# Sparse scores over stacked two-part operands, MLP up products grouped by part, tables in shared buffers, and a few unread products

## The chip, the cores and the metric

The kernel runs on one core of a Trainium2 chip. The metric is the device time of one execution in microseconds; the time of a kernel is the median of its runs.

## The reference, cut to what matters

The program computes, for one sequence of 256 positions and a width of 1024, three blocks one after another, each with a mixer and an MLP: a first block (softmax attention with a forget gate beside retention, with an adaptive norm from a condition vector), a block with sparse attention beside a pooling mixer, and a block with gated linear attention. All inputs are float32. The MLPs, and the sparse attention that the change rewrites, are:

```python
def sqrelu_mlp(x, w1, w2):                      # w1 1024x4096, w2 4096x1024
    return jnp.square(jax.nn.relu(x @ w1)) @ w2
...
q = h[..., :o1]...                              # 8 heads of 64, in 2 groups
k_cmp, v_cmp, k_slc, v_slc, k_win, v_win = ...  # of each group
kc = compress_blocks(k_cmp, ...)                # 15 compressed keys
s_c = jnp.einsum('bghqd,bgcd->bghqc', qb, kc)   # compressed scores
s_s = jnp.einsum('bghqd,bgqnd->bghqn', qb, k_sel)
s_w = jnp.einsum('bghqd,bgkd->bghqk', qb, k_w)
o = gb[..., 0:1] * o_c + gb[..., 1:2] * o_s + gb[..., 2:3] * o_w
```

With 256 positions there are four selectable blocks and all four are chosen, so the selected and the window branch are both causal attention over the whole sequence, with keys of their own.

## The kernel before, in words

Weights stream through a ring of six raw tiles of 128 x 1024 (SyncE issues the loads). Each tile is split in two float32r parts so that three fast products stand for one of full precision: ScalarE copies the rounded high part (`hi_to`, L591), VectorE subtracts it from the raw tile for the low part (`raw_to`, L1105), three tiles ahead of TensorE. The activations are split in the same way after a transpose (`quarter_hi`, `quarter_lo`). The products are a·hi, a·lo and b·hi (`three`, L1762 to L1766). In the MLP's `up` (L1889 to L1907), which runs for 15 of 16 steps of each of three MLPs, in two halves of four row blocks and two column blocks, a high weight block meets both parts of the activation in one product of 512 columns (L1903) and the low weight block the high part in one of 256 (L1905), in turn. `down` follows with `three` and 512 columns. The first of the 16 steps is `up_first`, with `three` and 256 columns.

The order of work is written out by hand: for every tile of a stage each engine has a list of steps (`tiles` on ScalarE and VectorE, `between` on TensorE), and semaphores tie them. GpSimd (POOL) makes reciprocal roots (`rsqrt`, L477) and issues loads of small tables in its program order; a wait ahead of one holds all that stand behind it. The modulation rows of the first block are summed on VectorE from raw tiles (L1115, L1131), and `mod_sums` on TensorE adds them up over the partitions, after which ScalarE and VectorE make the first activations.

The sparse stage begins at tile T_AIN (104). Its tiles come as keys (step 0 to 3), queries (4 to 7), window keys and gates (8 to 11, only 280 columns, so these tiles are short) and the pooling input (12 to 15). Steps that the change touches: `keys_out` and `block_out` copy the projections out of PSUM on ScalarE; `nsa_transposes(f)` turns them, f = 0, 1 for the compressed branch, 2 the selected keys, 3 to 6 the queries, 7 the window keys; `nt_out` and `q_out` copy these to `kT` and `qT` (64 rows per head). `block_keys`, `compress`, `hidden_bias`, `gelu_*`, `compress2` and `compressed_out` make the compressed keys; `cmp_scores`, `cmp_max`, `cmp_exp`, `cmp_probs`, `cmp_transposes`, `cmp_out` and `cmp_values` their attention. The two other branches have 12 groups, n = 6 to 17: a group of the first row tile has four heads and 128 keys, one of the second two heads and 256 keys. For each: scores `S_(n)` (`softmax_scores`, mask product L1986, score products L1993), `maxima(n)` on VectorE, `exps(n)` on ScalarE (L802), `weigh(n)` on VectorE, transposes `T_(n)` (L2005), a copy, values `V_(n)`. All groups from 6 on share one PSUM bank, so `S_(n)` waits for `exps(n-1)`. The pooled part goes to `uhi` and `ulo` and is the first operand of the out projection.

`busy` and `zeros` are products that nobody reads. `tab` holds first the retention's decay table and output gain, then the pooling bands.

```python
                        for kk in range(4):
                            k = 4 * half + kk
                            for f in range(2):
                                ...
                                mm(o, whi[:, s % SPL, c], hT[:, k, :, :].rearrange("p a s -> p (a s)"),
                                   start=k == 0, stop=False, skip_group_check=True)
                                ins = mm(o[:, 0:S], wlo[:, s % SPL, c], hT_hi[:, k, :], start=False, stop=k == KC - 1,
                                         skip_group_check=True)
                        ins.then_inc(w_used, 1)
```

## Time and profile before

| what | value |
|---|---|
| median of 3 runs | 1003.55 us (1002.07 to 1003.96) |
| the profiled execution | 1002.65 us |
| its span, first to last instruction | 1000.9 us |
| TensorE busy | 964.9 us, 96% of the span |
| VectorE, ScalarE, POOL busy | 670.9, 461.6, 53.9 us |
| mean granted TensorE clock | 0.989 |
| read from memory | 185.13 MB |

Times in the rows are microseconds from the span's start. A busy share tells which engine is full, not what an edit is worth; that is read from the waits and from the distance between starts. A matmul's record shows its whole way through the array, so records overlap, and a float32 product stands as two records. L12 is line 12 of the kernel before.

### The profile page before, as it was taken

The numbers are of one execution on the slowest core, as the hardware profiler recorded it, in microseconds if no ns is written. First come the engines' busy times: TensorE is split into PE (matmuls) and PEld (weight loads), VectorE is DVE, ScalarE is ACT, GpSimd is POOL, SyncE is SP. The second block draws the span as 40 slices with busy tenths as digits, with TensorE's granted clock in tenths as the row PEclk, the third lists the DMA queues.
The fourth block names the chain that finished last, engine by engine and source line by source line (L and its number), as shares of the span: only waits on it lengthen the run. The fifth ranks groups of instructions, "written<-read, shape, count | busy, mean of one in ns | idle before, by whom it ended". The sixth has DMA issues, their size and how long they took to land.

```text
span 1000.9 us, 13615 instructions
## 1 busy us (share of the span) xinstructions
PE 964.9 (96%) x4944; PEld 793.1 (79%) x4944; DVE 670.9 (67%) x867; ACT 461.6 (46%) x706; POOL 53.9 (5%) x59
## 2 busy tenths in 40 slices
PE   9899999799999999999899999999999999999996
PEld 7777877688888887977688888887776888888885
DVE  5877898795566576566876655677643876655657
ACT  5477545464454354544344544443652535544441
POOL 3040101100000001000020000001000010000000
PEclk9999999999999999899999999999999999999999
DMA  9988667596555676421375556565353446556541
GB/s 290 338 233 289 209 246 256 178 299 210 186 171 192 204 251 163 127 83 44 106 239 190 186 189 207 173 194 176 116 159 92 151 144 232 185 192 209 170 147 42
DMA packets 109987, 186.88 MB, mean 187 GB/s; under 512 B 8696, under 2 KB 67088, under 8 KB 109920
## 3 DMA queue, kind: packets, MB, share of 16 engines
q1 hardware_dynamic: 104800, 177.33, 54.4%
q0 software_dynamic: 2592, 8.53, 3.0%
q10 hardware_dynamic: 2544, 0.35, 0.2%
q8 instruction: 31, 0.51, 0.2%
q14 instruction: 20, 0.16, 0.1%
HBM read 185.13 MB, written 1.05 MB: 186 GB/s over the span
## 4 chain that ended last, share of the span: by engine, by line
PE 77%; DVE 10%; DMA 4%; ACT 4%; issue 3%; POOL 2%; SPq 0%; POOLq 0%; DVEq 0%; ACTq 0%
PE AT L1903 16%; PE PJ L1764 14%; PE PJ L1765 13%; PE PJ L1766 13%; PE AT L1905 8%; DVE wlo L1105 3%; DMA raw<-in_w_in_dram 2%; POOL rstd L477 2%; PE AT L1993 1%; ACT whi L591 1%; PE AT L1750 1%; DMA raw<-in_w_out_dram 1%; DMA raw<-in_w_ada_dram 1%; DVE acc L1131 1%; PE AT L2005 1%
## 5 line engine op out<-in xcount | busy, mean ns | idle before, releaser
L1903 PE MATMUL AT<-hT,whi 128*128 128x512 f32 x720 | 256.2, 398 | 0.0
L1105 DVE TENSOR_TENSOR wlo<-raw,whi 128x1024 fp32r<-128x1024 f32 x144 | 173.4, 1221 | 53.1 <-ACT whi L591 52.3
L1905 PE MATMUL AT<-hT,wlo 128*128 128x256 f32 x720 | 202.1, 281 | 0.0
L1231 DVE TENSOR_TENSOR wlo<-raw,whi 128x1024 fp32r<-128x1024 f32 x144 | 169.6, 1220 | 0.0
L591 ACT ACTIVATE whi<-raw 128x1024 fp32r<-128x1024 f32 x144 | 146.6, 1054 | 46.3 <-DMA raw<-in_w_in_dram 32.7
L1764 PE MATMUL PJ<-whi,uhi 128*128 128x512 f32 x408 | 160.8, 394 | 0.6 <-DVE ulo L1587 0.2
L1903 PEld LDWEIGHTS AT<-hT,whi 128*128 128x128 f32 x720 | 135.3, 188 | 32.9
L1765 PE MATMUL PJ<-wlo,uhi 128*128 128x512 f32 x408 | 159.2, 390 | 0.0
L1766 PE MATMUL PJ<-whi,ulo 128*128 128x512 f32 x408 | 158.9, 389 | 0.0
L1764 PE MATMUL PJ<-whi,hT 128*128 128x512 f32 (+1 forms) x344 | 141.7, 412 | 5.8 <-DVE hT L1288 1.9
L1241 DVE TENSOR_TENSOR pr<-AT,pr 128x512 f32<-128x512 f32 x45 | 31.1, 691 | 172.2 <-ACT pr L646 172.2
L638 ACT ACTIVATE whi<-raw 128x1024 fp32r<-128x1024 f32 x144 | 140.9, 1049 | 0.7 <-DMA raw<-in_w_mlp_in_dram 0.4
L1905 PEld LDWEIGHTS AT<-hT,wlo 128*128 128x128 f32 x720 | 136.0, 189 | 1.5
L1765 PE MATMUL PJ<-wlo,hT 128*128 128x512 f32 (+1 forms) x344 | 134.4, 391 | 0.0
L1766 PE MATMUL PJ<-whi,hT 128*128 128x512 f32 (+1 forms) x344 | 134.3, 390 | 0.0
L646 ACT ACTIVATE pr<-AT 128x512 f32<-128x512 f32 x45 | 26.8, 595 | 176.9 <-PE AT L1905 176.9
L1764 PEld LDWEIGHTS PJ<-whi,uhi 128*128 128x128 f32 x408 | 76.6, 188 | 19.2 <-issue 2.5
L1766 PEld LDWEIGHTS PJ<-whi,ulo 128*128 128x128 f32 x408 | 76.6, 188 | 16.5
L1765 PEld LDWEIGHTS PJ<-wlo,uhi 128*128 128x128 f32 x408 | 76.6, 188 | 14.4 <-issue 0.2
L1764 PEld LDWEIGHTS PJ<-whi,hT 128*128 128x128 f32 x344 | 65.6, 191 | 24.8 <-issue 6.1
L1766 PEld LDWEIGHTS PJ<-whi,hT 128*128 128x128 f32 x344 | 65.8, 191 | 13.8
L1765 PEld LDWEIGHTS PJ<-wlo,hT 128*128 128x128 f32 x344 | 65.9, 192 | 12.6 <-issue 1.0
(313 smaller groups left out, 976.2 us busy)
## 6 DMA issues: line engine op xcount, KB each, us to landing
raw<-in_mlp_w_dram SPq DMA_DIRECT2D x128, 512.0 KB, 4.7
raw<-in_w_in_dram SPq DMA_DIRECT2D x32, 512.0 KB, 6.5
raw<-in_w_ada_dram SPq DMA_DIRECT2D x32, 512.0 KB, 5.5
raw<-in_w_mlp_in_dram SPq DMA_DIRECT2D x32, 512.0 KB, 4.8
raw<-in_w_mlp_out_dram SPq DMA_DIRECT2D x32, 512.0 KB, 4.7
raw<-in_c_w_in_dram SPq DMA_DIRECT2D x24, 512.0 KB, 4.5
raw<-in_w_ada_dram SPq DMA_DIRECT2D x32, 256.0 KB, 6.4
raw<-in_a_w_in_dram SPq DMA_DIRECT2D x12, 512.0 KB, 5.9
```

Source lines behind the costliest of these rows:

```text
L477: nc.gpsimd.tensor_tensor(rstd[:, col:col + n], stat[:, col:col + n], nhalf[:, 0:n], ALU.pow).then_inc(rstd_ready, 1)
L591: nc.scalar.activation(whi[:, s % SPL, :], raw_slot(r), ACT.Copy).then_inc(hi_done, 1)
L638: nc.scalar.activation(whi[:, s % SPL, :], raw_slot(r), ACT.Copy).then_inc(hi_done, 1)
L646: nc.scalar.activation(pr[:, 0, :].rearrange("p (f s) -> p f s", f=2), AT[:, up_banks(j), S:], ACT.Copy).then_inc(cross_out, 1)
L1105: tt(wlo[:, n % SPL, :], raw_slot(r), whi[:, n % SPL, :].bitcast(F32), ALU.subtract).then_inc(raw_done, 1)
L1231: tt(wlo[:, s % SPL, :], raw_slot(r), whi[:, s % SPL, :].bitcast(F32), ALU.subtract)\
L1241: tt(z, AT[:, up_banks(j), 0:S], z, ALU.add).then_inc(up_out, 1)
L1764: mm(o, a, hi, start=start, stop=False)
L1765: mm(o, a, lo, start=False, stop=False)
L1766: return mm(o, b, hi, start=False, stop=stop)
L1903: mm(o, whi[:, s % SPL, c], hT[:, k, :, :].rearrange("p a s -> p (a s)"), start=k == 0, stop=False, skip_group_check=True)
L1905: ins = mm(o[:, 0:S], wlo[:, s % SPL, c], hT_hi[:, k, :], start=False, stop=k == KC - 1, skip_group_check=True)
```

## The change

It has these parts. (1) Sparse scores: queries and keys are laid out doubled (each head's 64 columns twice), so that a transpose gives 128 rows; the high part is copied to all rows, and for the queries VectorE overwrites rows 64 to 127 with the low part (`q_low`), so a stack of high and low part lies over 128 rows; for the keys, high and low part are two arrays, each twice over the rows (`k_low`). A score is then two float32r products over 128 rows. Queries lie in `uhi`/`ulo`, keys in the new `kst`, compressed keys in `kcst`, padded to 16 columns. The compressed steps move by one or two tiles, and S_9 is put ahead of T_7. (2) `up` makes the eight products of 512 columns of a half, then the eight of 256. (3) `tab` is gone: the decay table and the output gain go to `kT`, loaded after the fox scores, the bands to `qT`, loaded after the second norm's transposes; the pooled part goes to `hT`. (4) Unread products are also issued ahead of the first MLP's norm, in that MLP's start, and around `mod_sums`.

```diff
-        tab = sb("tab", [P, 1536])
+        kst = sb("kst", [P, 4, 512], F32R)
...
+        decay, rgain, bands = kT[:, 0:1024], kT[:, 1024:1536], qT[:, 0:1536]
...
-            bcast(rgain, dram["ret_out_gain"].rearrange("a h d -> (a h d)")).then_inc(ld_mix, 16)
-            pool.dma_start(tab[:, 0:1024], dram["decay_c"]).then_inc(ld_mix, 16)
             for t in range(NT):
                 rsqrt(S_FO + 8 * t, 8)
+            pool.wait_ge(at_mm, NF)
+            pool.dma_start(decay, dram["decay_c"]).then_inc(ld_tab, 16)
+            bcast(rgain, dram["ret_out_gain"].rearrange("a h d -> (a h d)")).then_inc(ld_tab, 16)
             for t in range(NT):
                 rsqrt(S_RO + 4 * t, 4)
             pool.wait_ge(src_ready, units(2))
-            pool.dma_start(tab[:, :], dram["bands_c"]).then_inc(ld_tab, 16)
...
+            pool.wait_ge(tr_done, units(3))
+            pool.dma_start(bands, dram["bands_c"]).then_inc(ld_tab, 16)
...
+            def queries_out():
+
+                act.wait_ge(w_used, T_AIN + 8)
+                for t in range(NT):
+                    nc.scalar.activation(
+                        acc[:, QD + D * t:QD + D * (t + 1)].rearrange("p (h a d) -> p h a d", h=8, a=2),
+                        bank(B_AIN + 1, t).rearrange("p (h d) -> p h d", h=8).unsqueeze(2).broadcast_to([P, 8, 2, 64]),
+                        ACT.Copy, scale=0.125).then_inc(bank_free[(B_AIN + 1) % 2], 1)
...
+            def q_low(f):
+
+                t, j = (f - 3) // 2, (f - 3) % 2
+                dve.wait_ge(nt_done, f + 1)
+                own = q_tile(j, t)[64:P]
+                tt(own, AT[64:P, 2 + f % 2, :].rearrange("d (h s) -> d h s", h=4), own.bitcast(F32), ALU.subtract)\
+                    .then_inc(nt_lo, 1)
+
+            def k_low(f, br):
+
+                dve.wait_ge(nt_done, f + 1)
+                tt(kst[:, K_HI[br] + 1, :], AT[:, 2, :], kst[:, K_HI[br], :].bitcast(F32), ALU.subtract).then_inc(nt_lo, 1)
...
+                kc = AT[:, 0, 64:94].rearrange("p (g c) -> p g c", g=2)
+                nc.vector.tensor_copy(kcst[:, :, :, NCMP:16], nhalf[:, 0:4].rearrange("p (a g c) -> p a g c", a=2, g=2))\
+                    .then_inc(c2_done, 1)
+                nc.vector.tensor_copy(kcst[:, 0, :, 0:NCMP], kc).then_inc(kc_hi, 1)
+                dve.wait_ge(kc_hi, 1)
+                tt(kcst[:, 1, :, 0:NCMP], kc, kcst[:, 0, :, 0:NCMP].bitcast(F32), ALU.subtract).then_inc(c2_done, 1)
...
             tiles(T_AIN, T_AOUT, {
-                5: [block_keys], 7: [gelu_start], 8: [gelu_end], 9: [compressed_out],
+                5: [block_keys, lambda: k_low(2, 0)], 7: [gelu_start], 8: [gelu_end, lambda: q_low(3), lambda: q_low(4)],
+                9: [compressed_out, lambda: q_low(5), lambda: q_low(6)],
                 10: [lambda: maxima(6)],
-                11: [gates_out, lambda: weigh(6), lambda: maxima(7), cmp_max],
-                12: [lambda: maxima(8), lambda: probs_out(6), cmp_probs, lambda: weigh(7)],
-                13: [lambda: maxima(9), lambda: probs_out(7), lambda: weigh(8)],
+                11: [gates_out, lambda: weigh(6), lambda: maxima(7)],
+                12: [lambda: maxima(8), lambda: probs_out(6), lambda: weigh(7), cmp_max],
+                13: [lambda: k_low(7, 1), lambda: maxima(9), lambda: probs_out(7), cmp_probs, lambda: weigh(8)],
...
-                        for kk in range(4):
+                        blocks = [(kk, f) for kk in range(4) for f in range(2)]
+                        c = lambda kk, f: slice(kk * FFB + f * P, kk * FFB + (f + 1) * P)
+                        out = lambda f: AT[:, up_banks(j), :][:, f, :]
+                        for kk, f in blocks:
                             k = 4 * half + kk
...
+                            mm(out(f), whi[:, s % SPL, c(kk, f)], hT[:, k, :, :].rearrange("p a s -> p (a s)"),
+                               start=k == 0, stop=False, skip_group_check=True)
+                        for kk, f in blocks:
+                            k = 4 * half + kk
+                            ins = mm(out(f)[:, 0:S], wlo[:, s % SPL, c(kk, f)], hT_hi[:, k, :], start=False, stop=k == KC - 1,
+                                     skip_group_check=True)
                         ins.then_inc(w_used, 1)
...
-                busy(3, 1) if m else None
+                busy(3, 1)
                 transposes(stage, 1, src)
-                busy(3, 2) if m else None
+                busy(3, 2 if m else 1)
                 up_first(0, 0)
-                busy(3, 4) if m else None
+                busy(3, 4)
...
+                    for part in range(2):
+                        k0 = S * (h // 4)
+                        ins = mm(o, q_stack(h)[:, rows_of(t)], kst[:, K_HI[br] + part, k0:k0 + kw], start=False, stop=part == 1,
+                                 skip_group_check=True)
...
                 if b == FIRST_BLOCKS - 1 and i < BLK - 1:
+                    zeros(2, 1)
                     mod_sums(i + 1)
+                    zeros(1, 1)
...
+            def gated_first():
+
+                busy(3, 4)
+                transposes(2, 0, from_q, [(mod_row, 6)])
...
+                if 4 <= f < 7:
+                    pe.wait_ge(nt_lo, f - 3 if f > 4 else 1)
...
             def nsa_scores(n):
                 if n == NF:
-                    pe.wait_ge(nt_done, 7)
+                    pe.wait_ge(nt_lo, 5)
+                if n == NF + 6:
+                    pe.wait_ge(nt_lo, 6)
...
-                10: [lambda: S_(6), lambda: cmp_scores((0,))],
-                11: [lambda: S_(7), lambda: cmp_scores((1,))],
-                12: [lambda: T_(6), lambda: S_(8)],
-                13: [lambda: V_(6), lambda: nsa_transposes(7), lambda: T_(7), cmp_transposes, lambda: S_(9)],
-                14: [cmp_values, lambda: V_(7), lambda: T_(8), lambda: S_(10)],
-                15: [lambda: V_(8), lambda: T_(9), lambda: S_(11), pool_bands, lambda: V_(9), lambda: T_(10), lambda: S_(12),
+                10: [lambda: S_(6)],
+                11: [lambda: S_(7), lambda: cmp_scores((0,))],
+                12: [lambda: T_(6), lambda: S_(8), lambda: cmp_scores((1,))],
+                13: [lambda: V_(6), lambda: nsa_transposes(7), lambda: S_(9), lambda: T_(7)],
+                14: [lambda: V_(7), cmp_transposes, lambda: T_(8), lambda: S_(10)],
+                15: [cmp_values, lambda: V_(8), lambda: T_(9), lambda: S_(11), pool_bands, lambda: V_(9), lambda: T_(10), lambda: S_(12),
```

## Rows read from the trace of the kernel before

**Rows 1.** The page: shares of the chain, a costly group, a load's median.

```profile
PE 77%; DVE 10%; DMA 4%; ACT 4%; issue 3%; POOL 2%; SPq 0%; POOLq 0%; DVEq 0%; ACTq 0%
...
L1903 PE MATMUL AT<-hT,whi 128*128 128x512 f32 x720 | 256.2, 398 | 0.0
...
raw<-in_w_in_dram SPq DMA_DIRECT2D x32, 512.0 KB, 6.5
```

**Rows 2.** Timeline of TensorE, MLP: start, us, engine, line, op, tiles, shape, count.

```profile
195.53 0.28 PE L1764 MATMUL AT<-whi,hT 128*128 128x256 f32 x1
...
196.25 0.28 PE L1764 MATMUL AT<-whi,hT 128*128 128x256 f32 x1
...
249.61 0.40 PE L1903 MATMUL AT<-hT,whi 128*128 128x512 f32 x1
...
251.02 0.40 PE L1764 MATMUL PJ<-whi,uhi 128*128 128x512 f32 x1
...
252.41 0.39 PE L1764 MATMUL PJ<-whi,uhi 128*128 128x512 f32 x1
...
255.81 0.39 PE L1764 MATMUL PJ<-whi,uhi 128*128 128x512 f32 x1
```

**Rows 3.** Windows: busy us (count) of PE, PEld, DVE, ACT, POOL; clock; DMA; GB/s.

```profile
186.94:190.36 3.42, 3.32 (x10) 2.79 (x11) 3.20 (x6) 1.32 (x3) 0.00 (x0) 0.50 0.43 144
...
415.64:419.05 3.41, 3.41 (x14) 2.84 (x14) 1.22 (x1) 2.00 (x6) 0.00 (x0) 0.50 0.30 110
...
422.46:425.88 3.42, 3.42 (x10) 2.68 (x9) 1.12 (x3) 1.49 (x8) 0.00 (x0) 0.50 0.00 0
```

**Rows 4.** Timeline of TensorE: a fox group, compressed scores, a sparse group.

```profile
90.98 0.27 PE L1986 MATMUL AT<-negb,identb 128*128 128x256 bf16 x1
...
92.19 0.40 PE L1765 MATMUL PJ<-wlo,hT 128*128 128x512 f32 x1
...
413.60 1.85 PE L2266 MATMUL AT<-sc,qT 64*128 64x15 f32 x16
...
440.48 0.27 PE L1986 MATMUL AT<-negb,identb 128*128 128x256 bf16 x1
...
442.08 0.40 PE L1765 MATMUL PJ<-wlo,hT 128*128 128x512 f32 x1
```

**Rows 5.** Timelines of TensorE and VectorE at the first block's second norm.

```profile
187.04 1.11 PE L1750 MATMUL AT<-cst,qT 128*128 128x128 f32 x4 [2.26 <-DVE qT L1469]
...
190.65 0.69 DVE L1182 TENSOR_TENSOR sc<-PJ,acc 128x512 f32<-128x512 f32 x1 [0.47 <-PE PJ L1766]
```

**Rows 6.** The chain in order of time: start, us, what.

```profile
74.94 8.30 DMA raw<-in_w_in_dram
...
167.51 9.06 DMA raw<-in_w_out_dram
```

**Rows 7.** Timelines around the first sparse scores: VectorE, TensorE, ScalarE.

```profile
409.12 0.21 DVE L1521 COPY proj<-sc 64x120 f32<-64x120 f32 x1
410.01 1.23 DVE L1105 TENSOR_TENSOR wlo<-raw,whi 128x1024 fp32r<-128x1024 f32 x1 [0.67 <-ACT whi L591]
...
411.25 0.67 DVE L1529 TENSOR_TENSOR proj<-AT,cst 120x512 f32<-120x512 f32 x1
...
412.28 0.39 PE L1986 MATMUL AT<-negb,identb 128*128 128x512 bf16 x1
...
415.56 0.37 ACT L802 ACTIVATE pr<-AT,nmax 128x128 f32<-128x128 f32 x1
```

**Rows 8.** Timelines: TensorE's waits behind late loads; POOL's and the decay's places.

```profile
90.52 0.63 PE L2005 MATMUL AT<-cst,pr 128*128 128x128 f32 x4 [1.19 <-ACT kT L783]
...
127.02 2.01 POOL L477 TENSOR_TENSOR rstd<-stat,nhalf 128x8 f32<-128x8 f32 x1 [13.39 <-DVE stat L1162]
...
144.81 0.42 DVE L1403 TENSOR_TENSOR pr<-AT,tab 128x256 f32<-128x256 f32 x1
...
179.04 0.50 PE L1764 MATMUL PJ<-whi,hT 128*128 128x512 f32 x1 [1.32 <-DVE wlo L1105]
```

More of the change, by code:

```diff
@@ L204, in block_program @@
         wsm2 = sb("wsm2", [P, KC, 32], F32R)
-        lfT = sb("lfT", [16, S])
+        lfT = rows[0:16, 1, 0:S]
         cvec = sb("cvec", [P, 4, KC])
@@ L892, in _, with keys_twice, window_out @@
                 hi_to(T_AIN + 3) if q == 1 else None
+            def keys_twice(src, t):
+                nc.scalar.activation(acc[:, KD + 256 * t:KD + 256 * (t + 1)].rearrange("p (g a d) -> p g a d", g=2, a=2),
+                                     src.rearrange("p (g d) -> p g d", g=2).unsqueeze(2).broadcast_to([P, 2, 2, 64]), ACT.Copy)
+            def queries_out():
[5 more added lines that the diff above has]
+                        ACT.Copy, scale=0.125).then_inc(bank_free[(B_AIN + 1) % 2], 1)
+            def window_out():
+                act.wait_ge(w_used, T_AIN + 12)
+                for t in range(NT):
+                    keys_twice(bank(B_AIN + 2, t)[:, 0:128], t)
+                    nc.scalar.activation(proj[:, t, 1152:1304], bank(B_AIN + 2, t)[:, 128:280], ACT.Copy)\
+                        .then_inc(bank_free[B_AIN % 2], 1)
             def keys_out():
@@ L1814, in out_first @@
                         bank_wait(pb + h, t)
-                    ins = tile_part(bank(pb + h, t), s0 + q, t, u4(uhi), u4(ulo), KPT * i, start=i == 0)
+                    ins = tile_part(bank(pb + h, t), s0 + q, t, u4(uhi) if hi is None else hi, u4(ulo) if lo is None else lo, KPT * i,
+                                    start=i == 0)
                 ins.then_inc(w_used, 1)
@@ L2170, in _, with zeros @@
             }
-            def zeros(n):
+            def zeros(n, b=3):
                 for _ in range(n):
-                    mm(AT[:, 3, 0:S], rows[:, 0, 0:P], rows[:, 0, 0:S], start=True, stop=True)
+                    mm(AT[:, b, 0:S], rows[:, 0, 0:P], rows[:, 0, 0:S], start=True, stop=True)
             pe.wait_ge(zeroed, 1)
@@ L2334, in pool_bands @@
                     u = lambda t: proj[:, t, N_U + P * g:N_U + P * (g + 1)]
-                    mm(o, u(0), tab[:, 384 * g:384 * g + S], start=True, stop=False)
-                    ins = mm(o[:, P:S], u(1), tab[:, 384 * g + S:384 * (g + 1)], start=False, stop=True)
+                    mm(o, u(0), bands[:, 384 * g:384 * g + S], start=True, stop=False)
+                    ins = mm(o[:, P:S], u(1), bands[:, 384 * g + S:384 * (g + 1)], start=False, stop=True)
                     if g % 2:
```

106 lines of the change are left out of this document (54 added, 52 removed).

## The prediction

> **What bounds the kernel now.** I read the page first, for shares: of the chain that ended last TensorE makes 77%, VectorE 10%, transfers and ScalarE 4% each [rows 1]. So an edit pays if it shortens TensorE's stream or one of the few waits in it. The reader should next look at starts, not durations: a matmul's shown duration is longer than the step to the next one. In the timeline of TensorE 15 products of 512 columns start in 3.40 us, 0.227 us each; in the MLP's up loop four pairs (512 columns, then 256) start in 1.41 us, 0.353 us a pair; where only 256-column products follow each other, six steps take 0.72 us, 0.120 us each [rows 2]. Then come the stretches by windows, for the granted clock: two short stretches of the sparse mixer and one at the end of the first out projection ran at 0.50, that is at 1.2 GHz [rows 3]; ahead of those in the mixer TensorE had run the score products of 15 columns [rows 4], ahead of the third it had stood idle [rows 5]. Last, the chain in order of time shows where TensorE waited, and two links are transfers of weights [rows 6].
>
> All sums are against the profiled execution's own time, 1002.65 us (span 1000.9). The median of the three runs is 1003.55, 0.9 higher; I add that at the end.
>
> **1. Up products by parts.** Nothing is added or removed: each of the 720 pairs [rows 1] keeps both products, but eight of 512 columns now stand ahead of eight of 256. A pair in pure runs would take 0.227 + 0.120 = 0.347 us, 0.0065 less than now; of the 8 pairs in each of the 90 half steps I leave one at today's price for the two seams, so 630 x 0.0065 = **-4.1 us**. The MLPs have no idle TensorE to hide it in. Bounds: 0 if the seams or the short runs eat it, -5.5 at best. What a run of short products costs is limited by its weight loads; the row that has exactly this (256 columns, new weights each time) is 0.120. A rule speaks against this part. The Trainium skill, "TensorE: Matmul & The Clock Gate", section "Part 3" (The mechanism), says that a weight load overlaps a running product only if it goes to other row groups. By that rule and the page's estimate for a load of 128 columns (107 ns) a 256-column product could not step below some 214 ns in either order, and this part would give 0. The trace steps at 120 ns [rows 2], so the measurement decides against it.
>
> **2. Sparse scores.** Now each head's product is float32 over 64 rows and runs as two records. A group of the second tile (two heads, 256 keys) takes from the mask product to the second product of the next tile 442.08 - 440.48 = 1.60 us; the same group of the first mixer, over 104 rows, 92.19 - 90.98 = 1.21 [rows 4]. So 0.39 of it is the change to the 64-row form and back. The new form has 128 rows and float32r: of the 1.21, 0.35 are the mask product and the first product of the tile, the rest four records of 0.215; with four passes of 0.120 for them it is 0.83, so 0.77 is saved in each of 8 groups: -6.2. A group of the first tile (four heads, 128 keys) swaps 8 records for 8 passes. No float32r product under 256 columns is in the trace. From below, 16 records of 15 columns take 1.85 us with the last one's tail, some 0.112 each [rows 4]; from above, a float32 record of 256 columns takes 0.215. I take 0.115, since the nearest row (128 columns of weights, short stream) is the first; that is no gain beyond the border cost, -0.36 in three groups (the fourth, S_13, stands ahead of a wait that ends on VectorE): -1.1. The compressed scores swap 32 records for 32 passes at the same floor: 0. Sum **-7.3**, bounds -8 and -3.9 (all 32 short passes at 0.215).
>
> What it adds is on the other engines. ScalarE copies the queries twice as wide (2 x some 0.45 more) and three small key copies: all before tile 7's compression, whose 64 products hide it. VectorE gets q_low four times and k_low twice. Not in the trace at 64 partitions; a 512-column VectorE operation from PSUM takes 0.67 [rows 7], bounds 0.4 and 0.7; I take 0.67. Here is the new wait. Today the gelu's last operation ends on VectorE at 409.33 [rows 7]. q_low(3) then ends at 410.0 and q_low(4) at 410.6; transposes 5, which TensorE reaches at some 409.1, now wait for the first, transposes 6 for the second: TensorE loses 0.9. Behind q_low(4) VectorE has the split of tile 12 (1.23 [rows 7]) and compressed_out, which waits for compress2 (itself later) and takes 1.2 with its new copies; only then q_low(5) and (6), done at 414.5. S_6 needs all four: it started at 412.28 [rows 7], TensorE would be there at 413.2, so 1.35 more. S_7 needs the exponentials of S_6, which now end 415.93 - 412.28 = 3.65 us after S_6's start [rows 7]; with the compressed scores moved behind S_7 only S_6 itself (1.3) and tile 11 (12 steps of 0.130 for 280 columns) lie between: 0.7. S_8 likewise waits for the exponentials of S_7, behind window_out and the gates on ScalarE: 0.7. T_7 waits for k_low(7), but S_9 now stands ahead: 0.1 more than today. T_8 waits for weigh(8), since VectorE has k_low and the moved cmp_probs ahead of it: 0.5. The waits add **+4.3**, bounds +2 and +7. Later steps have a microsecond of slack each and keep it.
>
> **3. Table loads moved.** The decay table and gain (128 x 1536 x 4 bytes, 768 KB) leave the stretch behind 72 us, where a weight load takes 8.30 us against a median of 6.5 for its kind, is on the chain, and ends in TensorE idle of 1.19 [rows 1, 6, 8]. The bands (768 KB) leave the stretch behind 166 us, where one takes 9.06 and leads to idle of 1.32 [rows 6, 8] and to the late start of the norm behind it. What can come back is 1.8 and 2.6 us of landing. In the first TensorE can use only its idle: **-1.2** (0 to -2.2). In the second VectorE's chain into the norm is what ends the stage, so I take **-1.9** (0 to -2.6). Where they go: POOL issues the first two behind its rsqrt that ends at 129.03; VectorE needs the table at 144.81 [rows 8], 15.8 us later, and POOL's next work, the rsqrt of the retention, comes behind that. The bands go behind the second norm's transposes, where POOL has only its wait for the next mixer ahead of it and the table is due two hundred microseconds later. Both take bandwidth from weights there; cover is the three tiles that the splits run ahead, and without it up to +1.
>
> **4. Products nobody reads.** Ahead of the first norm TensorE idles 2.26 us [rows 5]; the four busy products (0.87) lie in it, as do those in the MLP's start, where the next wait is as long. The gain is that VectorE's wait for the last product at 190.65 goes, 0.47 [rows 5], if the clock stays up: **-0.3** (0.2 to -1). At the start the three zeros around each mod_sums lie in idle twice; the third time TensorE comes to mod_sums without idle, and the next rows of h follow from it, so two zeros of 0.215 go on the path: **+0.4** (0 to 0.9).
>
> **5. The clock in the sparse mixer.** Each of the two low stretches of 3.4 us costs half of it, 1.7, where TensorE is the limit [rows 3]. The new scores fill the rows, but the 16-column products stay, in one cluster of S_7 and one of S_8, and TensorE now idles ahead of them. I take **-1.0** (+2 to -3.4).
>
> Sum: -4.1 - 7.3 + 4.3 - 1.2 - 1.9 - 0.3 + 0.4 - 1.0 = -11.1. 1002.65 - 11.1 = 991.55, and 0.9 more to stand beside a median: **992.4**.
>
> **Rivals.** (A) The order of the up products is worth nothing: seams and weight loads cost what the alternation costs. For it: a 256-column step is 13 ns over its stream already. Against: pure runs show 0.120. 992.4 + 4.1 = 996.5. This is also the time that the skill's rule gives, whose premise the trace denies. Chance 0.18. (B) The table loads were hidden: another link (ScalarE's head copies, VectorE's adds to the modulation sums) takes the place of the late weights. 992.4 + 3.1 = 995.5. For it: VectorE's adds to the modulation sums fill much of that stage. Chance 0.14. (C) Short float32r passes run at the float32 step: 32 x 0.10 = +3.3, 995.7. Chance 0.12. (D) Two of these together, 999: 0.05. (E) The clock holds through the mixer and VectorE's waits are half as long: -3.5 or so, 989: 0.09. (F) Slower: the waits of VectorE's subtractions ahead of S_6 to T_8 leave TensorE so thin that the clock stays at 1.2 GHz for all 28 us between; half of that is lost, +14, and the -1.0 does not come: 1007.5. It decides from some 24 us of low clock there. Against: today only two stretches of 3.4 us are low, one behind each cluster. Chance 0.03. The forecast as summed has 0.39.
>
> **Numbers.** 0.2% (2.0 us) is about what a measurement of this kernel tells from no change. All cases but F end below 1001.5 unless errors add up: faster 0.92, same 0.05, slower 0.03. Range 987.5 to 998: from E with its size errors to between D and the single rivals.
>
> **What would show it.** Right: the first product of each up half repeats at 0.227 eight times, then 0.120; a half in 2.78 us instead of 2.82; a second-tile score group near 0.83; no transfer of 8 or 9 us on the chain at 75 and 167; S_6 preceded by a wait for VectorE's qT-low subtraction of 1 to 2 us. Wrong: an unchanged 0.353 average per pair (A), TensorE still idle ahead of 90 and 179 us (B), 0.2 us steps in S_6 (C), windows at 0.50 one after another behind S_6 (F).

## The result, and the profile after

The changed kernel takes 992.60 us, median of 4 runs (991.15 to 994.73), against 1003.39 us for the kernel before on the same chip; the ratio is 0.9895, 95% interval 0.9874 to 0.9916. The profiled execution's span is 989.2 us against 1000.9, so 11.7 us were to be explained; the forecast had 11.1, and 992.4 for the median. First, the page of the changed kernel: engines, the clock by fortieths of the span, and the chain (its first line answers to [rows 1]).

```profile
span 989.2 us, 13707 instructions
PE 958.2 (97%) x4982; PEld 797.0 (81%) x4982; DVE 675.2 (68%) x875; ACT 463.4 (47%) x710; POOL 55.0 (6%) x61
...
PEclk9999999999999999999999999999999999999998
...
PE 78%; DVE 11%; ACT 3%; issue 3%; DMA 2%; POOL 2%; SPq 0%; POOLq 0%; DVEq 0%; ACTq 0%
```

TensorE's share rose and the transfers' share of the chain fell from 4% to 2%. Where the time went is read by the start of the same product (counted along TensorE's stream) in both traces; the last column is the difference.

| the same product | before, us | changed, us | changed - before |
|---|---|---|---|
| in projection, ahead of the decay load's old place | 86.35 | 86.17 | -0.18 |
| behind the late weight at 90 us | 97.33 | 95.46 | -1.88 |
| behind the retention's norm | 143.10 | 142.87 | -0.24 |
| in the first out projection | 173.03 | 172.81 | -0.21 |
| behind the late weight at 179 us | 180.53 | 178.73 | -1.81 |
| first up product, first MLP | 200.16 | 197.76 | -2.40 |
| behind the first MLP | 363.45 | 359.89 | -3.56 |
| sparse in projection | 392.30 | 388.78 | -3.52 |
| first product of the sparse mixer's out projection | 457.14 | 450.63 | -6.51 |
| first up product, second MLP | 507.48 | 498.02 | -9.45 |
| behind the second MLP | 670.36 | 659.76 | -10.60 |
| first up product, third MLP | 818.84 | 808.41 | -10.43 |
| last up products | 969.70 | 958.15 | -11.55 |

TensorE in the first MLP's up loop, timeline (start, us, engine, line, op, tiles, shape, count), which answers to [rows 2]:

```profile
197.76 2.00 PE L1956 MATMUL AT<-hT,whi 128*128 128x512 f32 x8
199.60 1.12 PE L1960 MATMUL AT<-hT,wlo 128*128 128x256 f32 x8
200.55 0.60 PE L1938 MATMUL AT<-cst,pr 128*128 128x128 f32 x4
```

Eight pairs take 200.55 - 197.76 = 2.79 us. The windows of the places that had a low clock before, and of one that had not; busy and count of PE, PEld, DVE, ACT, POOL, then the clock, the share of DMA and GB/s. They answer to [rows 3]:

```profile
136.51:139.93 3.42, 3.42 (x14) 3.04 (x13) 3.42 (x4) 2.74 (x4) 0.00 (x0) 0.50 0.47 134
186.94:190.36 3.42, 3.42 (x25) 3.17 (x24) 3.35 (x6) 1.98 (x6) 0.00 (x0) 1.00 0.03 12
405.00:435.00 30.00, 26.22 (x171) 21.47 (x170) 22.56 (x48) 14.06 (x41) 0.00 (x0) 1.00 0.27 88
```

A low stretch is, from here on, one at a granted clock of 0.50, 3.4 us long or twice that (longer only at the very end of the span). None is left in the sparse mixer, and a new one stands at 136.51 us, behind the retention's norm: that is the step from -1.88 to -0.24 in the table. The late weights, in the chain in order of time; the second answers to [rows 6], and in place of the first (8.30 us) the chain now runs along TensorE:

```profile
73.28 0.23 PE PJ L1816
...
167.31 7.43 DMA raw<-in_w_out_dram
```

TensorE at the second norm, which answers to [rows 5]: of 2.26 us of idle time 0.51 are left, since the unread products fill the rest.

```profile
185.21 0.66 PE L1802 MATMUL AT<-cst,qT 128*128 128x128 f32 x4 [0.51 <-DVE qT L1502]
```

The sparse mixer, timelines of TensorE and VectorE (idle time ahead and what ended it in brackets); they answer to [rows 4, 7]:

```profile
406.70 1.24 PE L2312 MATMUL AT<-cst,acc 128*128 128x128 f32 x8 [1.01 <-DVE uhi L1547]
...
411.15 0.39 PE L2041 MATMUL AT<-negb,identb 128*128 128x512 bf16 x1 [0.91 <-DVE ulo L1547]
...
414.70 0.39 PE L2041 MATMUL AT<-negb,identb 128*128 128x512 bf16 x1 [0.74 <-ACT pr L811]
...
415.77 1.01 PE L2336 MATMUL AT<-kcst,uhi 128*128 128x16 f32 x8
416.63 1.04 PE L2336 MATMUL AT<-kcst,ulo 128*128 128x16 f32 x8
417.53 0.48 PE L1816 MATMUL PJ<-whi,hT 128*128 128x512 f32 x1
...
428.92 0.66 PE L2065 MATMUL AT<-cst,pr 128*128 128x128 f32 x4 [0.83 <-DVE kst L1553]
...
433.98 0.27 PE L2041 MATMUL AT<-negb,identb 128*128 128x256 bf16 x1
434.01 0.72 PE L2052 MATMUL AT<-kst,ulo 128*128 128x256 f32 x4
434.56 0.39 PE L1816 MATMUL PJ<-whi,hT 128*128 128x512 f32 x1
434.79 0.39 PE L1817 MATMUL PJ<-wlo,hT 128*128 128x512 f32 x1
```

```profile
408.55 0.17 DVE L1575 CAST kcst<-nhalf 128x4 fp32r<-128x4 f32 x1
...
409.08 0.68 DVE L1580 TENSOR_TENSOR proj<-AT,cst 120x512 f32<-120x512 f32 x1
409.79 0.69 DVE L1547 TENSOR_TENSOR uhi<-AT,uhi 64x512 fp32r<-64x512 f32 x1
410.40 0.69 DVE L1547 TENSOR_TENSOR ulo<-AT,ulo 64x512 fp32r<-64x512 f32 x1
```

A second-tile group takes 434.79 - 433.98 = 0.81 us instead of 1.60. (Starts, not durations, are subtracted.) Ahead of it stand the waits that the change brought: transposes 5 for q_low(3), S_6 for q_low(6), which ends behind the compressed keys' copies, S_7 for the exponentials of S_6. A first-tile group, before and changed, from its mask product to the pooling product behind it:

```profile
450.93 0.38 PE L1986 MATMUL AT<-negb,identb 128*128 128x512 bf16 x1
...
452.32 0.48 PE L2344 MATMUL PJ<-proj,acc 128*128 128x256 f32 x1
```

```profile
444.66 0.38 PE L2041 MATMUL AT<-negb,identb 128*128 128x512 bf16 x1
...
445.72 0.43 PE L2416 MATMUL PJ<-proj,acc 128*128 128x256 f32 x1
```

### The profile page after: what moved, and what is told of

Its sections match the earlier page's. It is cut to its first block, busy times and chain, and to the rows that moved or that the text cites. A ratio compares the mean times of both kernels' runs of the same rounds, so it can differ in the third digit from the quotient of the medians.

```text
span 989.2 us, 13707 instructions
## 1 busy us (share of the span) xinstructions
PE 958.2 (97%) x4982; PEld 797.0 (81%) x4982; DVE 675.2 (68%) x875; ACT 463.4 (47%) x710; POOL 55.0 (6%) x61
## 4 chain that ended last, share of the span: by engine, by line
PE 78%; DVE 11%; ACT 3%; issue 3%; DMA 2%; POOL 2%; SPq 0%; POOLq 0%; DVEq 0%; ACTq 0%
PE AT L1956 16%; PE PJ L1816 14%; PE PJ L1817 14%; PE PJ L1818 14%; PE AT L1960 8%; DVE wlo L1137 3%; POOL rstd L483 2%; ACT whi L600 1%; PE AT L1802 1%; DVE bn L1225 1%; DMA raw<-in_w_out_dram 1%; DMA raw<-in_w_ada_dram 1%; PE AT L1816 1%; PE AT L2065 1%; DVE x L1223 1%
## 5 line engine op out<-in xcount | busy, mean ns | idle before, releaser
L1956 PE MATMUL AT<-hT,whi 128*128 128x512 f32 x720 | 179.5, 391 | 0.0
L1816 PE MATMUL PJ<-whi,uhi 128*128 128x512 f32 x392 | 154.0, 393 | 0.4
L1817 PE MATMUL PJ<-wlo,uhi 128*128 128x512 f32 x392 | 153.0, 390 | 0.0
L1818 PE MATMUL PJ<-whi,ulo 128*128 128x512 f32 x392 | 152.6, 389 | 0.0
L1956 PEld LDWEIGHTS AT<-hT,whi 128*128 128x128 f32 x720 | 131.9, 188 | 25.3
L1816 PE MATMUL PJ<-whi,hT 128*128 128x512 f32 (+1 forms) x360 | 146.7, 407 | 4.7 <-DVE hT L1320 1.6
L1817 PE MATMUL PJ<-wlo,hT 128*128 128x512 f32 (+1 forms) x360 | 139.6, 388 | 0.0
L1818 PE MATMUL PJ<-whi,hT 128*128 128x512 f32 (+1 forms) x360 | 139.5, 388 | 0.0
L1960 PEld LDWEIGHTS AT<-hT,wlo 128*128 128x128 f32 x720 | 98.2, 190 | 7.0
L1960 PE MATMUL AT<-hT,wlo 128*128 128x256 f32 x720 | 100.4, 282 | 0.0
L1816 PEld LDWEIGHTS PJ<-whi,hT 128*128 128x128 f32 x360 | 68.2, 189 | 22.2 <-issue 4.8
L1816 PEld LDWEIGHTS PJ<-whi,uhi 128*128 128x128 f32 x392 | 73.7, 188 | 15.2 <-issue 1.2
L1818 PEld LDWEIGHTS PJ<-whi,hT 128*128 128x128 f32 x360 | 68.0, 189 | 14.4
```

The source lines that it names most:

```text
L1816: mm(o, a, hi, start=start, stop=False)
L1817: mm(o, a, lo, start=False, stop=False)
L1818: return mm(o, b, hi, start=False, stop=stop)
L1956: mm(out(f), whi[:, s % SPL, c(kk, f)], hT[:, k, :, :].rearrange("p a s -> p (a s)"), start=k == 0, stop=False, skip_group_check=True)
L1960: ins = mm(out(f)[:, 0:S], wlo[:, s % SPL, c(kk, f)], hT_hi[:, k, :], start=False, stop=k == KC - 1, skip_group_check=True)
```

## The experiments

Each ratio is to runs of the kernel before on the same chip. One execution differs from the next by more than most terms here, so each run's trace is read too, by the same products as above.

**1. The changed kernel again**, without an edit.

> The changed kernel once more, with five rounds against the kernel before and a second profile. The first profile showed a low stretch of the TensorE clock at 136.51 us that the kernel before did not have, and none in the sparse mixer, where the kernel before had two. If these places belong to the kernel, the second profile shows the same (low stretches near 17, 136 and 983 us, none between 390 and 455) and the ratio is 0.989 to 0.990. If they shift from one execution to the next, the stretch at 136 is missing or one stands elsewhere, and the span moves by 1.7 us for each.

Measured: 993.06 us, ratio 0.9904 (0.9880 to 0.9927). Low stretches at 28.1, 137.3 and 983.8 us, none in the mixer. The stretch at 137 was there again, the early one had moved. That looked like a property of the kernel; run 11 shows that it isn't.

**2. The order of the up products alone**, in the kernel before (the products are written short here).

```diff
-                        for kk in range(4):
-                            for f in range(2):
-                                mm(o, whi ..., 512 columns)
-                                mm(o[:, 0:S], wlo ..., 256 columns)
+                        blocks = [(kk, f) for kk in range(4) for f in range(2)]
+                        for kk, f in blocks:
+                            mm(out(f), whi ..., 512 columns)
+                        for kk, f in blocks:
+                            mm(out(f)[:, 0:S], wlo ..., 256 columns)
```

> The kernel before with the order of the up products alone. My theory (both lengths run at the price of pure runs, seams aside): a half step of 8 pairs goes from 2.82 to 2.78 us, 90 half steps, -3.6 to -4.1 us, ratio 0.996. Rival A (the order is worth nothing, the 3.6 us seen between the two traces came from something else): 0 us, ratio 1.000. On the clock: all that comes before 200 us is unchanged, and from there on the mixer starts 1.2 us earlier; if the two low stretches of the sparse mixer hang on the products before them, they are still there.

Measured: 999.64 us, ratio 0.9961 (0.9942 to 0.9981). In the trace the difference to the kernel before goes from 0.23 to -0.85 us over 224 pairs of the first MLP, from -2.47 to -3.56 in the second and from -3.57 to -4.69 in the third: 1.09 us for 224 pairs, 3.5 for all 720. It grows evenly through each MLP. Rival A fell. One low stretch (419.6 us) was left in the mixer that the edit doesn't touch, where the kernel before had shown two.

**3. The table loads alone**, moved in the kernel before.

```diff
-            bcast(rgain, ...).then_inc(ld_mix, 16)
-            pool.dma_start(tab[:, 0:1024], dram["decay_c"]).then_inc(ld_mix, 16)
             for t in range(NT):
                 rsqrt(S_FO + 8 * t, 8)
+            pool.wait_ge(at_mm, NF)
+            pool.dma_start(tab[:, 0:1024], dram["decay_c"]).then_inc(ld_tab, 16)
+            bcast(rgain, ...).then_inc(ld_tab, 16)
...
             pool.wait_ge(src_ready, units(2))
-            pool.dma_start(tab[:, :], dram["bands_c"]).then_inc(ld_tab, 16)
...
+            pool.wait_ge(tr_done, units(3))
+            pool.dma_start(tab[:, :], dram["bands_c"]).then_inc(ld_tab, 16)
```

> The kernel before with the decay table, the gain and the bands loaded at the later places, into the buffer they had. My theory: TensorE's waits ahead of 90 and 179 us go, -1.7 and -1.6 us in the trace, -3.1 to -3.3 in all, ratio 0.9968. Rival B (these gains came with something else of the change): 0 to -1, ratio 0.999 or more. If the low clock stretch behind the retention norm (136 us in the changed kernel) comes with the earlier start of that norm, it shows here too and takes back 1.6: -1.6, ratio 0.9984.

Measured: 1002.80 us, ratio 0.9983 (0.9961 to 1.0005): by the times, inconclusive. The trace says more. TensorE's idle time ahead of 90 us is gone, worth 1.61 (difference 1.13 to -0.48). Behind the norm a low stretch at 138.2 us took 1.58 of it back. The second weight came in only a little sooner, and TensorE still waited for it (chain, then timeline; [rows 6, 8] have 9.06 and 1.32):

```profile
168.64 8.61 DMA raw<-in_w_out_dram
```

```profile
179.72 0.50 PE L1767 MATMUL PJ<-whi,hT 128*128 128x512 f32 x1 [0.87 <-DVE wlo L1107]
```

That is 0.45, and a low stretch at 196 us ate it. In the eight profiles that have this load moved together with the rest of the change, the same weight took 7.4 to 8.2 us; in the three with the old place 9.0 to 9.1. So the direction is shown; how much of the second gain belongs to the bands alone is not, from one profile.

**4. The compressed branch alone at its later places**, in the kernel before.

```diff
-                10: [lambda: S_(6), lambda: cmp_scores((0,))],
-                11: [lambda: S_(7), lambda: cmp_scores((1,))],
-                12: [lambda: T_(6), lambda: S_(8)],
+                10: [lambda: S_(6)],
+                11: [lambda: S_(7), lambda: cmp_scores((0,))],
+                12: [lambda: T_(6), lambda: S_(8), lambda: cmp_scores((1,))],
```

and cmp_max, cmp_exp, cmp_probs, cmp_out, cmp_transposes and cmp_values one tile later, as in the change.

> The kernel before with the compressed branch alone at its later places: the 16 float32 score products of a tile behind the next score group, with what hangs on them on VectorE and ScalarE. Theory 1 for the clock of the sparse mixer (it fell because two clusters of 15-column products on 64 rows stood close behind each other): with S_6 ahead of no cluster and both clusters one score group later, one low stretch or two remain, 0 to -1.7 us. Theory 2 (the order of the steps decides, the rows that a product fills do not): no low stretch is left in the mixer, -3.4 us, ratio 0.9966. Theory 3 (rows filled decide): both are still there, moved by some 3 to 5 us, 0 us.

Measured: 1004.72 us, ratio 1.0016 (0.9997 to 1.0035), one low stretch in the mixer, at 420.7 us. Across the mixer the difference to the kernel before is 1.38 us at both ends. This fits theory 1, but the theories were no test: run 2, whose mixer is untouched, had one stretch as well, so "one left" tells nothing. Inconclusive for the clock. The order alone isn't free, though: with one low stretch fewer the mixer should have come out some 1.6 us shorter, and it is as long as before. TensorE has new idle time ahead of S_7, which waits for the exponentials, and ahead of T_8, where VectorE's weighing now stands behind its steps for the compressed branch:

```profile
417.47 0.39 PE L1986 MATMUL AT<-negb,identb 128*128 128x512 bf16 x1 [0.60 <-ACT pr L802]
...
439.57 0.63 PE L2005 MATMUL AT<-cst,pr 128*128 128x128 f32 x4 [0.64 <-issue]
```

So waits of 1.2 us at S_7 and T_8 come with the moved compressed branch, without any of VectorE's new subtractions.

**5. q_low(5) and (6) ahead of the compressed keys' copies**, in the changed kernel.

```diff
-                9: [compressed_out, lambda: q_low(5), lambda: q_low(6)],
+                9: [lambda: q_low(5), lambda: q_low(6), compressed_out],
```

> The changed kernel with one list turned round: VectorE takes the low parts of the last two query transposes ahead of the copies of the compressed keys. In the changed kernel's trace these copies lie at 408.55 to 409.79 us, q_low(6) ends at 411.1, and S_6 starts at 411.15 after 1.07 us of waiting. My theory (the wait ahead of S_6 is VectorE's queue and nothing else): S_6 comes 1.0 us earlier, S_7 keeps its own wait of 0.9 and comes 1.0 earlier too, and so does the start of the next out projection. Rival 1: another wait takes its place at once (the bank of tile 10, the exponentials): under 0.3. Rival 2: it is given back further on, at S_8, T_7 or T_8, where VectorE and ScalarE are no earlier: S_6 -1.0, but the out projection's start 0 to -0.3. All read against the changed kernel's own trace, from the step of tile 9 on.

Measured: 995.17 us, ratio 0.9910 (0.9876 to 0.9944). TensorE:

```profile
411.96 0.39 PE L2041 MATMUL AT<-negb,identb 128*128 128x512 bf16 x1
...
416.20 0.39 PE L2041 MATMUL AT<-negb,identb 128*128 128x512 bf16 x1 [1.43 <-ACT pr L811]
```

VectorE, and the clock by windows:

```profile
412.19 0.68 DVE L1580 TENSOR_TENSOR proj<-AT,cst 120x512 f32<-120x512 f32 x1
412.79 1.21 DVE L1137 TENSOR_TENSOR wlo<-raw,whi 128x1024 fp32r<-128x1024 f32 x1
413.92 0.68 DVE L1376 TENSOR_REDUCE nmax<-AT 128x4 f32<-128x512 f32 x1
```

```profile
417.54:424.37 6.83, 6.83 (x24) 5.96 (x24) 3.22 (x8) 2.22 (x12) 0.00 (x0) 0.50 0.25 77
```

This execution is 1.88 us behind the changed kernel's first profile ahead of the mixer. Against that, S_6 came 1.07 earlier, as forecast, with no wait. S_7 came only 0.38 earlier: its idle time grew from 0.74 to 1.43 us. The copies that I had moved away from S_6 now stand, with a split, ahead of the maxima of S_6, and S_7 waits for the exponentials behind them. Rival 2 in kind, one step sooner than I had put it. A low stretch of 6.83 us began 1.3 us behind the start of S_7. At the out projection's start this execution is 4.45 us behind the changed kernel's, so the mixer lost 2.57 us where the theory had a gain of 1.0. Whether the longer wait brought the low clock isn't shown: runs 8, 9 and 11 have a low stretch that begins at 418.0 us too, without the longer wait.

**6. Seven products that nobody reads** ahead of the retention's last turn, in the changed kernel.

```diff
                 busy(0, 5) if f == 2 else None
+                busy(3, 7) if f == 3 else None
                 pe.wait_ge(rope_done, f + 1)
```

> The changed kernel with seven more products that nobody reads, ahead of the last of the retention's four turns, where TensorE stands idle for 1.66 us. Theory (the low clock stretch at 136.51 us in the changed kernel, and at 137 to 138 us in three other profiles, follows that idle time): no low stretch between 130 and 145 us, and from 140 us on the kernel is 1.6 us earlier against the same point of the changed kernel; median near 991.5. Rival: the low stretch stays or moves to the next thin place, and the products add 0 to 0.2.

Measured: 994.06 us, ratio 0.9912 (0.9881 to 0.9944), so by the times no gain on the changed kernel. TensorE:

```profile
134.03 3.19 PE L1812 MATMUL AT<-cst 128*128 128x256 f32 x14
137.05 0.60 PE L2173 MATMUL AT<-cst,proj 128*128 128x128 f32 x4
```

No low stretch, but the turn 1.2 us late: a float32 product is two records, so seven are 14 and take 3.0 us, in a gap of 1.66. I had counted seven. In the trace the gain against the changed kernel is 0.44 us instead of 1.6.

**7. The two table loads cut to 8 columns**, in the changed kernel (so the decay and the band weights are left out of what is computed).

> The changed kernel with its two table loads cut to 8 of their columns (the decay table and the bands are left out of the computation, their place and their waits stay). Theory (at their new places the loads are hidden): the stretches 129 to 142 and 182 to 230 us are as long as in the changed kernel, within 0.2 each. Rival: they slow the weights there, and without them the norm ahead of 198 us or the retention comes 0.5 to 1.0 earlier.

Measured: 992.64 us, ratio 0.9887 (0.9856 to 0.9917). Between 130 and 174 us the difference to the changed kernel moves only by the low stretch that this execution hadn't (3.27 to 1.64); from 175 to 206 us it goes from 1.62 to 1.50. The loads cost 0.1 at their new places: hidden, as the prediction had it.

**8. Without the busy products at the end of the first out projection and in the first MLP's start**, in the changed kernel.

```diff
-                busy(3, 1)
+                busy(3, 1) if m else None
...
-                busy(3, 4)
                 transposes(2, 0, from_q, [(mod_row, 6)])
```

> The changed kernel without the products that nobody reads at the end of the first out projection and in the start of the first MLP. Theory (they keep the clock up there): a low stretch stands between 183 and 200 us, as in the kernel before, and the first up product comes 0.5 to 1.4 us later than in the changed kernel. Rival (they fill idle time and do nothing): no low stretch, 0 to -0.2.

Measured: 993.24 us, ratio 0.9900 (0.9869 to 0.9931). The first up product comes 0.7 us later than the changed kernel's by the same count (-0.52 to 0.19), and a low stretch is there:

```profile
185.90:189.31 3.41, 3.41 (x13) 2.72 (x12) 3.30 (x6) 1.33 (x4) 0.00 (x0) 0.50 0.24 97
```

But 0.57 of the 0.7 is there at 180 us already, ahead of the products: the weight took 7.99 us in this execution and not 7.43. What is left for the products is 0.14. The stretch is real and cheap: 0.80 us behind at 189 us has become 0.19 at 195, since TensorE's wait for VectorE at 192.48 us, still 1.71 us long in this run, takes up the rest.

**9 and 10. The order around the waits**, and the same with three busy products ahead of the last turn.

```diff
-                9: [compressed_out, lambda: q_low(5), lambda: q_low(6)],
-                10: [lambda: maxima(6)],
-                11: [gates_out, lambda: weigh(6), lambda: maxima(7)],
+                9: [lambda: q_low(5), lambda: q_low(6)],
+                10: [lambda: maxima(6), compressed_out],
+                11: [lambda: maxima(7), gates_out, lambda: weigh(6)],
...
-                11: [lambda: S_(7), lambda: cmp_scores((0,))],
-                12: [lambda: T_(6), lambda: S_(8), lambda: cmp_scores((1,))],
-                13: [lambda: V_(6), lambda: nsa_transposes(7), ...
+                11: [lambda: cmp_scores((0,)), lambda: S_(7)],
+                12: [lambda: T_(6), lambda: S_(8), lambda: cmp_scores((1,)), lambda: nsa_transposes(7)],
+                13: [lambda: V_(6), ...
```

with nt_out(7) and k_low(7) one tile earlier too, and in run 10 also busy(3, 3) where run 6 had 7.

> The changed kernel with the order around its waits changed: q_low(5) and (6) first, then the maxima of S_6, then the compressed keys' copies; the first 16 compressed products ahead of S_7 instead of behind it, where TensorE waited 0.9 us for S_6's exponentials (1.72 us when only q_low was moved); the maxima of S_7 ahead of the gates; the last key transposes and k_low one tile earlier, so that T_7 doesn't wait for k_low. Theory: S_6 -1.0, S_8 -1.7, T_7 and the start of the out projection -2.7 against the same steps of the changed kernel, and no low clock stretch between 405 and 435 us, since the idle time ahead of S_7 is gone. Rival 1 (the chain of VectorE and ScalarE through the exponentials of S_6 and S_7 sets S_8, whatever stands on TensorE): S_6 -1.0, but S_8 only -0.5, the out projection -1.5. Rival 2: the thin stretch lets the clock fall as in the run with q_low moved alone, +1.6 to +3.4.

> The same with three products that nobody reads ahead of the retention's last turn (seven ran as 14 records in 3.0 us and came out 1.2 us late; three make 6 records, 1.3 us, inside the 1.66 us that TensorE stands idle there). Theory: no low stretch between 130 and 145 us, the turn at its old time, -1.6 against a changed kernel that has the stretch and 0 against one that has not; with the -2.7 of the order some 989. Rival: the stretch is still there, or what it gives is lost at another thin place; then it is as the run without them.

Measured: 992.06 us, ratio 0.9881 (0.9854 to 0.9908), and 989.82 us, ratio 0.9866 (0.9843 to 0.9890). TensorE of run 10:

```profile
137.39 1.46 PE L1812 MATMUL AT<-cst 128*128 128x256 f32 x6
139.12 0.66 PE L2173 MATMUL AT<-cst,proj 128*128 128x128 f32 x4 [0.27 <-DVEq L1429]
...
411.83 0.39 PE L2041 MATMUL AT<-negb,identb 128*128 128x512 bf16 x1
...
414.83 1.06 PE L2337 MATMUL AT<-kcst,uhi 128*128 128x16 f32 x8 [0.19 <-DVE proj L1580]
...
416.65 0.39 PE L2041 MATMUL AT<-negb,identb 128*128 128x512 bf16 x1
...
427.90 0.60 PE L2065 MATMUL AT<-cst,pr 128*128 128x128 f32 x4
```

S_6, S_7 and T_7 no longer wait; the 1.0 us ahead of transposes 5 is still there. Against the changed kernel's first profile, run 10 goes from 1.76 us at 394 us to -0.92 at the out projection's start: -2.68, forecast -2.7. Run 9 goes from 2.17 to 0.95 with a low stretch at 418 us between; 1.2 gained and some 1.5 given to the clock. So the theory on the order held (S_8 came 1.70 us earlier in run 10, as forecast), and rival 1, the chain of VectorE and ScalarE, fell. The theory's clause on the clock fell in run 9, where rival 2's 1.6 came: the low stretch comes without idle time ahead of S_7 too. Run 10 has the same order there and no stretch. Run 10 is the fastest kernel of the study, 2.95 us under the changed kernel on the same chip (run 11). The intervals overlap; the 2.7 us rest on the traces. Its median also has whatever the three products at the turn give.

**11. The changed kernel a third time.**

> The changed kernel a third time, on the chip of the two kernels above, to compare medians and to see its low stretches once more. If the places seen so far belong to the kernel: low near 137 us, none between 390 and 455 us. If they shift from one execution to the next: one of the two is otherwise. Ratio to the kernel before 0.989 to 0.991.

Measured: 992.77 us, ratio 0.9894 (0.9870 to 0.9919). Low stretches at 15.2, 73.2, 417.95 and 984.6 us: none at 137, one in the mixer. The places shift between executions of the same kernel. The mean granted clock of three stretches in all profiles (by windows; 1.00 is no low stretch, 0.96 one, 0.91 two in the last column):

| profile | 130 to 146 us | 146 to 200 us | 400 to 440 us |
|---|---|---|---|
| before | 1.00 | 0.97 | 0.91 |
| 2, up order alone | 1.00 | 0.97 | 0.96 |
| 3, loads alone | 0.89 | 0.97 | 0.96 |
| 4, compressed branch later | 0.89 | 0.97 | 0.96 |
| 8, changed, no busy products | 1.00 | 0.97 | 0.96 |
| changed; 1; 11 | 0.89; 0.89; 1.00 | 1.00; 1.00; 1.00 | 1.00; 1.00; 0.96 |
| 5, q_low first | 0.89 | 1.00 | 0.91 |
| 6, busy at the last turn | 1.00 | 1.00 | 1.00 |
| 7, no tables | 1.00 | 1.00 | 1.00 |
| 9, order | 0.89 | 1.00 | 0.96 |
| 10, order and busy | 1.00 | 1.00 | 1.00 |

The middle column is the one that divides cleanly: low in all five profiles without busy products at the norm, never in the eight with them. In the first column 6 of 11 without filled idle time are low, neither of the two with it. In the last, four profiles with the old scores have five low stretches, nine with the new ones have five (the one of double length in run 5 counted as two).

## Why the prediction was right

The total was right to 0.6 us of the profiled pair (-11.7 against -11.1) and to 0.2 us of the median (992.60 against 992.4). The mechanisms of the two big gains and of the waits were right too, and the chosen case, the sum as it stood, is the one that came. But some terms were off and cancelled, and that part is luck: the up products gave 0.6 less than forecast and 0.5 of the mixer's gain is not in the table, while the waits cost 0.2 less, the loads gave 0.2 more, the norm 0.3, the clock 0.6 and the start 0.6.

**Up products.** Forecast -4.1. A half step takes 2.79 us where I had 2.78, the seams cost what I had left for them plus 0.01, and the whole is -3.5 (run 2; in the changed kernel's table -1.16 and -1.15 over the first and second MLP, and -1.12 over 224 pairs of the third). Most of the miss is in my arithmetic, not in the chip: unrounded, the rows give 1.41/4 - 3.40/15 - 0.72/6 = 0.0058 us a pair [rows 2], not 0.0065, and 630 x 0.0058 is -3.7. The rule of the Trainium skill that I had weighed ("TensorE: Matmul & The Clock Gate", section "Part 3") would have made it 0; eight products of 256 columns with new weights each start 0.12 us apart here (1.12 us for the eight with the last one's tail), so the measurement decides against it once more.

**Sparse scores.** Forecast -7.3 for the products. A second-tile group went from 1.60 to 0.81 (I had 0.83); a first-tile group from 452.32 - 450.93 = 1.39 to 445.72 - 444.66 = 1.06 (I had -0.36, it is -0.33); the 32 compressed passes take 1.76 us for 16, from 415.77 to 417.53, against 1.78 before, which is the 0 that I had. Eight groups at -0.79 and three at -0.33 make -7.3. That includes the border to the 64-row form and back, which I had inferred from a group over 104 rows. Rival C fell: float32r passes of 16 and 128 columns start 0.11 us apart (its 32 x 0.10 is 3.2, not 3.3, which changes nothing).

**The waits.** Forecast +4.3. Transposes 5 and 6 lost 1.4 (I had 0.9), S_6 1.07 (1.35), S_7 0.9 (0.7), S_8 0.2 (0.7), T_7 0.15 (0.1), T_8 0.4 (0.5): 4.1 in all. Named in the right places and of the right size together. The biggest error is S_8: VectorE and ScalarE had caught up behind S_7. Run 5 shows that the one at S_6 came from VectorE's queue, and also that taking it away alone pushes the rest onto S_7; runs 9 and 10 show that 2.7 us of these waits are an order, not a price. Run 4 bears out the reasons that I had given for two of them: with the compressed scores behind S_7 and cmp_probs ahead of weigh(8), and nothing else of the change, TensorE waits 0.60 at S_7 and 0.64 at T_8.

**What the mixer's terms leave open.** From 392 to 507 us the table has -5.93. The terms as measured make -7.3 + 4.1 - 3.2 = -6.4, with the two low stretches at 1.6 each. Of the 0.5 left over, 0.4 is lost at the last score group: from its mask product to the second product of the next tile it takes 1.22 us, not 0.81, and TensorE's idle time ahead of the first of these two, 0.14 us, ends on VectorE. The rest was not followed up.

```profile
468.19 0.27 PE L2041 MATMUL AT<-negb,identb 128*128 128x256 bf16 x1
...
469.07 0.50 PE L1816 MATMUL PJ<-whi,hT 128*128 128x512 f32 x1
469.41 0.39 PE L1817 MATMUL PJ<-wlo,hT 128*128 128x512 f32 x1
```

**Table loads.** Forecast -1.2 and -1.9. The first gave -1.7 in the changed kernel and -1.6 alone (run 3); I had capped it at TensorE's idle time of 1.19 on one wait and had left out the shorter one behind it. The second gave -1.6 by 180 us in the first profile and 0.6 less where the weight took 8 us (run 8). Rival B fell for the first load; for the second, run 3 leaves open how much is the bands' own. At the new places they cost nothing (run 7).

**Products nobody reads.** At the norm -0.3 forecast, -0.14 by run 8: right in mechanism, the clock stays up, and small for the reason given, VectorE's pace. The pair shows -0.59 from 180 to 200 us (-1.81 to -2.40), and run 8 keeps 0.48 of it without these products (-1.73 to -2.21), so most of that is something else; the bands' new place is a candidate, and no run separates it. At the start I had +0.4; the difference to the kernel before at 66.76 us is -0.22 in the first profile and -0.4 to 0.3 in the others that have no low stretch past 30 us there, while runs 2 to 4, without these zeros, have 0.1 to 1.1. In the pair the kernel before has two low stretches there, the changed one has one. Such stretches at 15 to 36 us hide what the zeros do; no run was made on them alone, and the term stays open.

**The clock.** This is the step whose account was furthest from what the pair shows. I took -1.0 in the mixer; the profiled pair has -3.2 there (two stretches gone, 1.6 each by the same products, where I had 1.7) and +1.6 behind the retention's norm, a stretch at a place that I had not named. Neither is the change's doing for sure: run 11 has the changed kernel with the one in the mixer and without the other. As a mean over profiles the mixer went from 5 stretches in 4 to 5 in 9, about 0.7 fewer or 1.1 us, which is near the -1.0; on so few profiles this is an indication. What the runs without a trace add: the mean granted clock was 0.988 in 50 runs of the kernel before and in the runs of 2 and 3, and 0.9915 in 16 of the changed kernel. That is two stretches less by the estimate of 3.4 us at half clock each. One, at the norm, is in every profile; where the other lies, in the mixer, at the start or elsewhere, these means don't tell. Had the pair shown those -1.1 in the mixer and no stretch at 136 us in either, it would be -11.7 + 2.1 - 1.6 = -11.2; the medians differ by 10.8. So the total owes less to luck than its split does.

**The slower rival** (F) fell in the changed kernel. Run 5 comes nearest to it, with 6.83 us of low clock behind a longer wait, far from the 24 us that it needed.

## What to carry to other kernels

When a change adds work to a second engine inside a chain that feeds TensorE, list what stands ahead of it in that engine's queue: here 2.7 us of the new waits went by moving operations that nobody was waiting for behind those that somebody was. Ask also what stays on TensorE between two steps that hang on each other: run 4 paid 0.60 us at S_7 because 16 products had moved from in front of it to behind it. A wait can't be judged by taking away its last cause alone, since the next operation in that queue becomes the wait. And where a few tenths of a per cent decide, read several profiles of the same kernel: each low stretch of the clock moves up to 1.6 us, and its place changes from one execution to the next.

## What the runs showed that I had not expected

The places of the low stretches (0.50 of the clock, 1.2 GHz) change between executions of one kernel, as run 11 beside run 1 shows, and one costs what TensorE is worth where it falls: 1.6 us at 136.51 us, where TensorE sets the pace, 0.14 at most at the norm (run 8), where VectorE does. A late weight can hide one altogether. Run 4, with the table loads at their old place, lost 1.6 us to a stretch at 72.5 us (difference 0.11 to 1.71), and at 97 us the difference was -0.14: TensorE, being late, had not met the wait at 90 us [rows 8] at all. In run 5, with the loads moved, a stretch at 72.8 us cost the same 1.6, and 1.35 of it stayed. So part of what the moved loads save is given back in the executions that are slow ahead of them.
